# Opening by column blocks of x, and the MLP's up-projection with stationary weight tiles

## What is computed

```python
def rmsnorm(x, g):
    y = xf * lax.rsqrt(jnp.mean(xf * xf, axis=-1, keepdims=True) + EPS)
    return (y * g.astype(jnp.float32)).astype(x.dtype)

def sq_relu_mlp(hn, w1, w2):                 # w1 2048 x 8192, w2 8192 x 2048
    return jnp.square(jax.nn.relu(hn @ w1)) @ w2

for i in range(DEPTH):                       # 2 layers
    hn = rmsnorm(h, ln_mix[i])
    h = h + mamba2_mixer(hn, ...)            # layer 0: in_w 2048 x 10304, out_w 4096 x 2048
    ...                                      # layer 1: mla_mixer
    h = h + sq_relu_mlp(rmsnorm(h, ln_mlp[i]), mlp_w1[i], mlp_w2[i])
    h = per_layer_input(h, p[i], ple_norm[i], ple_gate_w[i], ple_proj_w[i])
```

## Time and profile before

| what | us |
|---|---|
| median of 3 executions | 2680.68 |
| lowest and highest | 2677.83, 2680.77 |
| the profiled execution, own time | 2678.15 |
| its span, first to last instruction | 2676.5 |

### The profile page before, as it was taken

How to read it: one execution, slowest core, us unless ns; L and a number is a source line. 1 busy time by engine, 2 the same in 40 slices (tenths; PEclk the granted TensorE clock), 3 DMA queues, 4 the chain that set the end, 5 groups by cost and what they waited for, 6 DMA issues and landing times.

```text
span 2676.5 us, 33247 instructions
## 1 busy us (share of the span) xinstructions
PE 2614.5 (98%) x12154; PEld 2166.6 (81%) x12154; DVE 1578.6 (59%) x1782; ACT 1266.2 (47%) x1503; POOL 119.7 (4%) x234
## 2 busy tenths in 40 slices
PE   7999999999999999999999997999999999999998
PEld 6888888888788888888888876878888888888887
DVE  5677777776855555555555665657555555545554
ACT  5655455545444443443445545645444434434453
POOL 0000000000000000000000004320000000000000
PEclk9999999999999999999999999999999999999999
DMA  6655666555466666656665543445666566666653
GB/s 207 192 180 176 196 190 188 186 180 180 151 191 188 194 184 191 189 184 196 188 187 181 187 142 103 128 136 179 187 190 191 185 195 186 189 192 188 186 181 125
DMA packets 251168, 479.63 MB, mean 179 GB/s; under 512 B 19882, under 2 KB 22964, under 8 KB 250804
## 3 DMA queue, kind: packets, MB, share of 16 engines
q1 hardware_dynamic: 246196, 464.78, 56.9%
q0 software_dynamic: 2880, 10.49, 1.2%
q10 hardware_dynamic: 1984, 2.85, 0.3%
HBM read 475.90 MB, written 2.16 MB: 179 GB/s over the span
## 4 chain that ended last, share of the span: by engine, by line
PE 91%; DVE 3%; issue 3%; ACT 1%; POOL 1%; DMA 0%; SPq 0%; ACTq 0%; POOLq 0%; DVEq 0%
PE acc L1382 28%; PE acc L1384 28%; PE acc L1383 28%; PE tp L1434 3%; DVE w_lo L939 1%; PE mid L1512 1%; ACT w_hi L552 1%; DVE xa_lo L956 0%; DVE tmp L965 0%; DMA scratch<-in_ssm_norm 0%; PE mid L1669 0%; PE mid L1668 0%; PE tp L1514 0%; ACT scratch L571 0%; POOL small L473 0%
## 5 line engine op out<-in xcount | busy, mean ns | idle before, releaser
L939 DVE TENSOR_TENSOR w_lo<-raw,w_hi 128x1024 fp32r<-128x1024 f32 x890 | 1081.8, 1221 | 980.6 <-ACT w_hi L552 980.5
L552 ACT ACTIVATE w_hi<-raw 128x1024 fp32r<-128x1024 f32 x890 | 933.3, 1055 | 1128.8 <-PE acc L1384 1128.7
L1382 PE MATMUL acc<-w_hi,xa_hi 128*128 128x512 f32 x2016 | 795.6, 395 | 5.6 <-DVE w_lo L939 2.5
L1384 PE MATMUL acc<-w_hi,xa_lo 128*128 128x512 f32 x2016 | 785.3, 390 | 0.0
L1383 PE MATMUL acc<-w_lo,xa_hi 128*128 128x512 f32 x2016 | 784.8, 389 | 0.0
L1382 PE MATMUL acc<-w_hi,ya_hi 128*128 128x512 f32 (+1 forms) x1504 | 592.1, 394 | 12.3 <-DVE w_lo L939 9.1
L1384 PE MATMUL acc<-w_hi,ya_lo 128*128 128x512 f32 (+1 forms) x1504 | 583.7, 388 | 0.0
L1383 PE MATMUL acc<-w_lo,ya_hi 128*128 128x512 f32 (+1 forms) x1504 | 583.4, 388 | 0.0
L1382 PEld LDWEIGHTS acc<-w_hi,xa_hi 128*128 128x128 f32 x2016 | 378.6, 188 | 85.6 <-issue 5.1
L1384 PEld LDWEIGHTS acc<-w_hi,xa_lo 128*128 128x128 f32 x2016 | 378.4, 188 | 79.4
L1383 PEld LDWEIGHTS acc<-w_lo,xa_hi 128*128 128x128 f32 x2016 | 378.8, 188 | 77.8 <-issue 1.7
(11 more groups left out here) (215 smaller groups left out, 1180.2 us busy)
## 6 DMA issues: line engine op xcount, KB each, us to landing
raw<-in_mlp_w SPq DMA_DIRECT2D x512, 512.0 KB, 3.7
raw<-in_ssm_in_w SPq DMA_DIRECT2D x161, 512.0 KB, 4.3
raw<-in_ssm_out_w SPq DMA_DIRECT2D x64, 512.0 KB, 3.7
raw<-in_ple_gate_w SPq DMA_DIRECT2D x64, 512.0 KB, 4.7
raw<-in_mla_out_w SPq DMA_DIRECT2D x32, 512.0 KB, 3.8
scratch<-cumulative POOLq DMA_DIRECT2D x16, 512.0 KB, 6.3
raw<-in_ple_proj_w SPq DMA_DIRECT2D x8, 512.0 KB, 4.5
raw<-in_w_dq SPq DMA_DIRECT2D x8, 512.0 KB, 4.3
```

Source lines behind the costliest of these rows:

```text
L552: act.activation(w_hi[:, g % SPL, :, 0:cols], raw[:, g % RAW, :, 0:cols], ACT.Copy)\
L939: dve.tensor_tensor(w_lo[:, g % SPL, :, 0:cols], raw[:, g % RAW, :, 0:cols], w_hi[:, g % SPL, :, 0:cols].bitcast(F32), ALU.subtract).then_ ...
L1382: pe.matmul(dst, xh, wh, start=first and k == 0, stop=False)
L1384: mm = pe.matmul(dst, xl, wh, start=False, stop=last and k == 1)
```

## The change

**Opening.** x comes in four transfers, one per block of 512 columns, each with a semaphore of its own. The first weights are chunk 0 of the first B unit; SyncE then loads the row of ln_mix alone, waits for block 1 of x before chunks 1 and 2, and for block 3 before chunks 3 to 7; the six small transfers that ScalarE issued follow. The other eleven rows are issued by POOL. The first B unit runs first, begun with block 0 alone; the dt columns come behind it, and every dt step one unit later. The work on x is spread over the jobs of that unit; one small ScalarE copy is put ahead of all.

**MLP up-projection.** `xa` is one tensor [128, K tile, 2, 256 tokens] with high and low part side by side. The weights are stationary in tiles of 128 K by 128 columns: for each, w_hi times [high | low] is one matmul of 512 columns into one PSUM bank, and w_lo times high one of 256 columns. The result has the features on the partitions, in four banks: two pairs out of "A", "B", "M" (`mid`) and "T" (`tp`), in turn. ScalarE copies the cross term (columns 256 to 511), VectorE adds the first half to it, then does relu and square in one instruction; high and low part of `ya` come from SBUF. The scale rstd^2 (made by POOL) is multiplied in where the down unit is added to h. The MLP's hardware loops are written out. The down units, gates, attention and scan keep their matmuls.

```diff
         h = sb("h", [P, NT, D])
-        xa = sb("xa_hi", [P, KT, TOK], F32R), sb("xa_lo", [P, KT, TOK], F32R)
+        xa_both = sb("xa", [P, KT, 2, TOK], F32R)
+        xa = xa_both[:, :, 0], xa_both[:, :, 1]
...
+        halves = {"A": acc_a[:, :, :], "B": acc_b[:, :, :], "M": mid_both[:, :, :],
+                  "T": tflat.rearrange("p (b n) -> p b n", b=2)}
...
@@ sync
+            first_chunk(0)
+            sp.dma_start(vrows[0:ln_mix.shape[0] * KT, 0], ln_mix.rearrange("l (a b) -> (l a) b", b=P))\
+                .then_inc(S["mix"], 16)
+            sp.wait_ge(s_x[1], 16)
+            first_chunk(1)
+            first_chunk(2)
+            sp.wait_ge(s_x[NB - 1], 16)
+            for k in range(3, KT // 2):
+                first_chunk(k)
...
@@ gpsimd
+                if n in (1, 4):
+                    own(last)
+                    last = pool.tensor_tensor(rstd_sq[:, n // 3], rstd[:, n], rstd[:, n], ALU.mult)
...
@@ scalar
-            for t in range(NT):
-                act.dma_start(h[:, t], x[0, t * P:(t + 1) * P, :]).then_inc(S["xin"], 16)
...
             for blk in range(NB):
-                act_hi(tiles(xa, blk), first_tmp[blk])()
-            split()
-            for blk in range(NB):
-                sums(0, blk, None)()
+                act.dma_start(h[:, :, c512(512 * blk)], x_in[:, :, c512(512 * blk)]).then_inc(s_x[blk], 16)
+            act.wait_ge(S["warm"], 1)
+            act.activation(junk[:, 0, 0:16], power[:, 0], ACT.Copy)
...
-            unit({2: [take_narrow(dt_t, "A", 0)], 3: [rope_sines], 5: [softplus]})
...
+            unit({0: [first_hi(0), x_sums(0)], 1: [first_hi(1), x_sums(1), first_hi(2)], 2: [first_hi(3), x_sums(2)],
+                  3: [x_sums(3)], 7: [rope_sines]})
...
-                    return {3: [take(lambda t: r_sb[:, t], pair, "r", ACT.Relu, n)],
-                            5: [act_hi(tiles(ya, j), src, "Tu")]}
+                def middle(j):
+                    def second_term(before):
+                        act.wait_ge(S["used"], before)
+                        for m, half in enumerate((pp[0] + "M", "T" + pp[1])[j % 2]):
+                            w.tick("r")
+                            act.activation(k_t[:, 2 * m:2 * m + 2], halves[half][:, :, TOK:2 * TOK], ACT.Copy)                                .then_inc(S["r"], 1)
+                    return {3: [second_term], 5: [act_hi(tiles(ya, j), q_t, "sq")]}
...
@@ vector
-            unit({0: [rope_angles], 3: [dt_row], 5: [dt_log]})
+            unit({0: [blocks((first_gain, 0), (first_gain, 1), (first_lo, 0), (first_gain, 2))],
+                  1: [blocks((first_lo, 1), (first_gain, 3), (first_lo, 2))],
+                  2: [blocks((first_lo, 3))], 4: [other_rows], 6: [rope_angles]})
+            rest()
...
+                        for m, half in enumerate((pp[0] + "M", "T" + pp[1])[j % 2]):
+                            on("r")
+                            v = k_t[:, 2 * m:2 * m + 2]
+                            signal(dve.tensor_tensor(v, halves[half][:, :, 0:TOK], v, ALU.add), "u")
+                        dve.wait_ge(S["u"], w.now("u"))
+                        signal(dve.scalar_tensor_tensor(q_t, k_t, 0.0, k_t, ALU.max, ALU.mult), "sq")
+                    return {3: [square], 5: [lo(tiles(ya, j), q_t)]}
...
+                        last = dve.scalar_tensor_tensor(v, acc[pair][t][:, :], rstd_sq[:, layer, t:t + 1], v,
+                                                        ALU.mult, ALU.add)
...
@@ tensor
+            for blk in range(NB - 1):
+                turn_x(blk)
+            unit(xa, "B", "xr", {0: [turn_last_x], 2: [turn_rows_of_weights]}, range(1, NB + 1))
+            narrow_chunk(xa, dt_psum)
...
-                def turn_middle():
-                    on("sq")
-                    hold("T", "act")
-                    flip(lambda j, t: sq_sb[:, t, P * j:P * j + P], feature, 4, NT).then_inc(S["Tu"], 1)
+                def up(j, jobs=None, need=None):
+                    for n in range(8):
+                        if need and n % 2 == 0:
+                            pe.wait_ge(S["act"], need[n // 2])
+                        g = w.tick("G")
+                        pe.wait_ge(S["lo"], g + 1)
+                        for f in range(4):
+                            half = (pp[0] + "M", "T" + pp[1])[j % 2][f // 2]
+                            if n == 0 and f % 2 == 0:
+                                hold(half, "u")
+                            dst = halves[half][:, f % 2]
+                            for k in range(2):
+                                wh, wl = (v[:, g % SPL, k, P * f:P * f + P] for v in (w_hi, w_lo))
+                                pe.matmul(dst, wh, xa_both[:, 2 * n + k].rearrange("p a t -> p (a t)"),
+                                          start=n == 0 and k == 0, stop=False)
+                                mm = pe.matmul(dst[:, 0:TOK], wl, xa_both[:, 2 * n + k, 0],
+                                               start=False, stop=n == 7 and k == 1)
+                        mm.then_inc(S["used"], 1)
```

More of the change, by code:

```diff
@@ L466, in _, with rows, row128 @@
             last.then_inc(S["setup"], 1)
+            def rows(column, vec):
+                pool.dma_start(vrows[column % P:column % P + vec.shape[0], column // P], vec)\
+                    .then_inc(S["vec"], 16)
+            def row128(v):
+                return v.rearrange("(a b) -> a b", b=P)
+            rows(V_MLP, ln_mlp.rearrange("l (a b) -> (l a) b", b=P))
+            rows(V_PLE, ple_norm.rearrange("l (a b) -> (l a) b", b=P))
+            rows(V_KVIN, row128(kv_in_norm))
+            rows(V_CKV, row128(ckv_norm))
+            rows(V_CQ, row128(cq_norm[0]))
+            rows(V_KN, row128(k_nope_norm))
+            rows(V_QN, row128(q_nope_norm[0]))
+            taps = ssm_conv_w[0].rearrange("k (a b) -> (k a) b", b=P)
+            rows(V_CONV, taps[0:P])
+            rows(V_CONV + P, taps[P:CONV_W * CONV_TILES])
+            rows(V_CONV + CONV_W * CONV_TILES, row128(ssm_conv_b[0]))
+            rows(V_SSM, row128(ssm_norm[0]))
             def root(src, n, dst):
@@ L967, in gain, with add_scaled, job @@
                 return job
+            def add_scaled(pair, blk, layer):
+                def job(before):
+                    dve.wait_ge(S["used"], w.at("G", before))
+                    for t in range(NT):
+                        v = h[:, t, c512(512 * blk)]
+                        last = dve.scalar_tensor_tensor(v, acc[pair][t][:, :], rstd_sq[:, layer, t:t + 1], v,
+                                                        ALU.mult, ALU.add)
+                    signal(last, "hadd")
+                return job
             def add(pair, blk, late=0):
@@ L997, in first_lo, with blocks @@
                 lo(tiles(xa, blk), first_tmp[blk])()
-            for step, blk in ((first_gain, 0), (first_gain, 1), (first_gain, 2), (first_lo, 0), (first_gain, 3),
-                              (first_lo, 1), (first_lo, 2), (first_lo, 3)):
-                step(blk)
-            rest()
+            def blocks(*steps):
+                return lambda before: [step(blk) for step, blk in steps]
             def rope_angles(before):
@@ L1167, in mlp, with middle @@
             def mlp(layer, pp, first):
-                def middle(pair, j):
+                def middle(j):
                     def square(before):
-                        on("r")
-                        signal(dve.tensor_tensor(sq_sb[:, :, :], r_sb[:, :, :], r_sb[:, :, :], ALU.mult), "sq")
-                    return {3: [square], 5: [lo(tiles(ya, j), tp[:, :, :])]}
+                        for m, half in enumerate((pp[0] + "M", "T" + pp[1])[j % 2]):
[5 more added lines that the diff above has]
+                    return {3: [square], 5: [lo(tiles(ya, j), q_t)]}
                 unit(first)
-                with w.rounds(3, MLP_ROUND):
+                for q in range(3):
                     for j in range(4):
-                        unit(middle(pp[j % 2], j))
+                        unit(middle(j))
+                    if q == 0:
+                        dve.wait_ge(S["rs"], 3 * layer + 2)
                     for j in range(4):
-                        unit({3: [add(pp[j % 2], j)]})
+                        unit({3: [add_scaled(pp[j % 2], j, layer)]})
                 for j in range(4):
-                    unit(middle(pp[j % 2], j))
+                    unit(middle(j))
                 for j in range(3):
-                    jobs = {3: [add(pp[j % 2], j)], 5: [gain(V_PLE + 16 * layer + 4 * j)], 6: [lo(tiles(xa, j))]}
+                    jobs = {3: [add_scaled(pp[j % 2], j, layer)], 5: [gain(V_PLE + 16 * layer + 4 * j)], 6: [lo(tiles(xa, j))]}
                     if j == 2:
@@ L1197, in gated @@
                     return job
-                unit({3: [add(pp[1], 3)]}, halves=4)
+                unit({3: [add_scaled(pp[1], 3, layer)]}, halves=4)
                 unit({1: [gain(V_PLE + 16 * layer + 12)], 4: [lo(tiles(xa, 3))]})
```

183 lines of the change are left out of this document (97 added, 86 removed).

## The result

| | before | changed | ratio (95% interval) |
|---|---|---|---|
| median of 5 runs each, us | 2680.68 (2677.83 to 2680.83) | 2664.83 (2662.96 to 2667.34) | 0.9945 (0.9931 to 0.996) |
| profiled execution, us | 2678.15 | 2664.7 | |
| its span, us | 2676.5 | 2663.1 | |

The change is faster by 15.9 us, 0.6%. I forecast 2650.0 us, 30.7 us faster, with a range that ended at 2663; the time lies 1.8 us above it. The sign is right, the size is not: of the forecast gain 52% came.

The account below looks back on a forecast made before the run. The prediction took TensorE's instructions, busy 98% of the span, as the bound. Its terms, -14.1 - 28.2 + 13.8 - 1.4 = -29.9 us, gave 2648.2 us from 2678.15, or 2650 us on the median's scale; range 2638 to 2663 us.

Parts of the forecast that it names:

- Opening: Start of the kernel: x in blocks lets TensorE start early, first unit ending at 42.0 instead of 56.1 us, -14.1 us.
- block 0 and the chunk are there at about 5.3 us: Opening: landing time of x block 0 and the first weight chunk, reckoned from 340 GB/s.
- they have a unit of 21.7 us as cover: Opening: dt steps moved one unit later stay hidden; without cover their waits, 3 to 4 us, would count once.
- Transposes: MLP up-projection: 32 units lose eight transposes each, 0.88 us a set, -28.2 us.
- Weight loads: MLP up-projection: 128 loads instead of 96, a unit 22.18 against 21.74 us, +13.8 us over 32 units.
- My bound of 3 ns per short matmul: MLP up-projection: uncertainty of the load price put into the range, 2048 x 3 ns = 6 us.
- Loops: MLP loop written out: two loop returns of 0.67 us in layer 0 go, -1.4 us.
- Work costed at nothing: MLP copies, PSUM additions, the scaled addition into h and POOL's square of rstd stay off TensorE's path, 0 us.
- A: MLP up-projection: short matmuls do not cover the next load, 188 instead of 120 ns each, +139 us, 2789 us; chance 0.05.
- B: Opening brings little: slow TensorE in first chunks, late rows from POOL, some 10 us less gain, 2660 us; chance 0.12.
- C: Written-out MLPs fetch instructions late: 0.67 us in each of 128 units, +86 us, 2736 us; chance 0.04.
- D: MLP: new chain through PSUM holds the down unit, 3 us at eight entries, +24 us, 2674 us; chance 0.05.

Follow-up runs that it names:

- experiment 5: The change with the first layer's mixing row (ln_mix) transferred ahead of weight chunk 0 instead of behind it: 2667.85 us, ratio 0.9961.
- experiment 6: The change with the jobs of the first unit behind the opening back in the order of the kernel before: 2663.34 us, ratio 0.9943.
- experiment 11: Change with matmuls grouped in twos, experiment 6's job order, VectorE's low weight chunk 2 before x block 2's, three ScalarE sums of squares later: 2655.18 us.
- experiments 2 and 3: The change with up-projection matmuls grouped, two long then two short (2657.09 us), or all eight long then eight short per chunk (2659.05 us).
- experiment 4: The change plus eight idle transposes behind chunk 1 of the first up unit in rounds two to four of each MLP: 2660.66 us, ratio 0.9928.
- experiment 9: The change plus only 20 idle transposes in TensorE's wait for the last scan group: 2664.62 us, ratio 0.9945.

## Why the prediction was wrong

**What bounds the kernel** held: TensorE's instructions, 98% of the span.

**Opening, forecast -14.1 us: 10.5 us by the ledger.** The first full matmul came at 13.41, not 11.5 us, and the unit behind the opening at 43.68, not 42.0 us: 1.7 us. The step that failed is "block 0 and the chunk are there at about 5.3 us", and with it "block 0 is turned by 7.3 us". In the trace the chunk lands at 6.30 us and block 0 at 6.71 us: up to 5.3 us the core moved 157 GB/s on average, 0.83 MB in all, less than the 1.05 MB of the two:

```profile
0.00:5.30 5.30, 0.00 (x0) 0.00 (x0) 0.00 (x0) 1.50 (x2) 4.33 (x53) 1.00 0.59 157
```

Block 0 was then turned from 7.23 us on, since TensorE's program has the row of `ln_mix` ahead of it, which landed at 6.9 us:

```profile
7.02 0.28 PE L1515 MATMUL acc_b<-ident,scratch 32*128 32x32 f32 x1 [7.02 <-DMA scratch<-in_ln_mix]
7.23 1.97 PE L1496 MATMUL tp<-ident,h 128*128 128x128 f32 x8
```

I had costed x and the weights, and not the 16 KB between them; but of the 1.9 us by which the transposes begin late, the row accounts for 0.5 us, from 6.71 to 7.23 us, and the landing of block 0 for the rest. That the row alone holds the kernel up is not shown, since experiment 5 brings it forward only by delaying the chunk.

The rest of the chain was close: chunk 2 follows chunk 0 by 7.66 us where I had 7.6 (forecast 19.1 us, seen 21.07), and there is no wait from chunk 3 on. Something else that I had put at nothing holds chunk 2 as well: chunk 1 of the weights is issued at 8.14 us, when block 1 of x has landed, and lands at 13.98 us. VectorE waits 0.54 us for its high part and has no gap from 15.10 us on, up to the low part of chunk 2. With the load where it is, an earlier chunk 0 alone would therefore not have moved chunk 2; in experiment 6 the load lands at 13.03 us and chunk 2 still follows chunk 0 by 7.64 us. VectorE's order, changed in experiment 11, moved it by 1.2 us.

From the unit behind the opening on, the gain falls from 12.96 to 10.49 us: 0.54 us are the two dt transposes that now come behind this mark, which the 56.1 us of my sum had left out; nearly all the rest is the new wait of 1.63 us at 68.69 us and the slower first matmul behind it: "they have a unit of 21.7 us as cover" was true of the length of the dt steps and false of their place in the queue, as experiment 6 shows for the order of that unit's jobs as a whole.

**Transposes, forecast -28.2 us: right.** A down entry after an up round gains 0.88 us in the ledger, and a unit of the first round gains 0.47 us, which is 0.88 less 0.41 for the loads. The Trainium skill's figure in "TensorE: Matmul & The Clock Gate", "Part 4: PE-mode transpose", would have given an estimated 70 us, and no part of the ledger has room for it.

**Weight loads, forecast +13.8 us: about +24 us.** This is the main error, two thirds of the miss. 64 x 226.5 + 64 x 120.0 ns gave the time of one unit in four (22.18 us seen), though not by its parts. The step that failed is taking two distances, each from a stream of one length, as the price of a stream that alternates them. That stream has a cycle of its own, 346.7 or 353.3 ns a pair, and ran in the longer for 24 of 32 units. My bound of 3 ns per short matmul, 6 us, was too narrow for it: 24 units of 64 pairs at 6.6 ns are 10 us. That the order decides is shown (experiments 2 and 3: 22.29 and 22.35 us a unit, in every round), that both cycles are stable under the same instructions too (experiment 4). Why the stream in rounds two to four is caught in the long one, and what in TensorE makes three pairs repeat, stays open.

**Loops, forecast -1.4 us: right.** In the kernel before, the two up units at a return of the loop take 45.13 and 45.09 us together, and 44.41 us at the round's start where no loop returns: 0.72 and 0.68 us.

**Work costed at nothing** was nothing: no wait of TensorE between 760 and 1380 us, on any engine.

**Not forecast:** the half clock at 691 us, net 1.7 us with the one at 1632 us that went.

The sum: 3.6 + 10.3 + 1.7 = 15.6 of the 15.8 us missing.

**The rivals.** A (the short matmul does not cover its load, 2789 us): not seen as stated. Its own threshold, 14.6 ns a short matmul, is far off; the long cycle costs 6.6. The rule of the Trainium skill named with it ("TensorE: Matmul & The Clock Gate", "Part 3: Packing small matmuls"), a load overlaps a matmul in flight only if the row group differs, does not describe this stream: 128 loads whose records last 188 ns each pass in 22.2 us, of which 20.4 us are columns by the distances of the prediction (64 x 213 + 64 x 106.5 ns). B (opening short by some 10 us): a third of it came, by other causes. C (instruction fetch): no gap marked "issue" in the MLPs; its price was reckoned with 128 MLP units, but there are 64 (32 up, 32 down), so one stop in each would be 43 us and not 86. D (PSUM chain): no wait for ya_lo in them.

## What to carry over

Price a new pattern of instructions by a stretch that has the same pattern; where the trace has none, add the distances of its parts and put at least 2% of the stream's time into the range, and try the order of long and short members by itself, since it costs nothing to change and was worth half as much as the rest of this change. When a step is moved into a unit with much spare time, look at which split stands behind it in its queue, and not at the unit's length. In an opening, ask when each transfer lands with all the others under way, the smallest too, and which of them is issued only when another has landed.

## What was not expected of the hardware

- Alternating matmuls of 512 and 256 columns with a 128-column load each run at 346.7 or at 353.3 ns a pair for whole rounds of four units, with the same instructions, clock and buffers; grouped in twos they take 348.3 ns, in eights 349.2 ns, in every round.
- After equal idle times (3.15 and 3.16 us) in front of the same work, the clock stayed at 2.4 GHz in one kernel and was granted at 1.2 GHz in the other; with the same program up to there, five traces had it at 1.2 GHz for 6.8 us (three) or 3.4 us (two). 20 transposes in the idle time were followed by full clock in three of three traces; in the attention part the half-clock stretches then came at other places (three against one in experiment 9), and the kernel's time did not move (2664.62 against 2664.83 us).
- With x and weights under way, 16 KB issued behind a 512 KB transfer landed 5.5 us after its issue, at 6.9 us; issued ahead of it (experiment 5), it landed 2.5 us after its issue, at 3.4 us, and the 512 KB at 7.8 instead of 6.3 us.
